# State-space stage and recurrent output path: the order of a feature tile's, a scan step's and an output's parts dealt anew

## The chip, the cores and the metric

The kernel runs on one core of a Trainium2 chip. It has TensorE (PE) for matrix products, VectorE (DVE), ScalarE (ACT) and GpSimd (POOL) for the rest, and SyncE (SP), which here only issues transfers. The metric is the device time of one execution in microseconds, the median of several.

## What is computed

Three blocks over a sequence of 1024 positions and 1024 features, in float32: a gated linear attention block with an MLP, a hybrid block (state-space and differential attention), and a block with a convolution and a gated recurrence. The change touches the state-space half of the second block and the recurrence of the third. Of the reference, cut:

```python
# second block, state-space half
z, xbc, dt_f, dt_b, q, k, v, g = jnp.split(h @ w_in, offs, axis=-1)
xbc = silu(centred_dwconv(xbc, conv_w, conv_b))            # 5 taps, 1536 features
xs, Bm, Cm = split(xbc)                                    # 1024, 2 x 128, 2 x 128
# ssd_chunked, both directions; chunks of 128, 16 heads of 64 in 2 groups
a_cs = cumsum(dt * A)
decay = exp(where(lower, a_cs[l] - a_cs[s], -inf))
y_diag = einsum(cb[..., None] * decay, x * dt)             # cb = C B^T
chunk_states = einsum(Bm, x * dt * decay_to_end)
prev = scan(dec * h + st)                                  # over 8 chunks
y_off = einsum(Cm, prev) * exp(a_cs)
y = y_fwd + y_bwd + D * xs
y_ssm = rms_norm(y * silu(z))                              # per group
# third block, recurrence: 8 heads of 128, y_hgrn = rms_norm(o) * silu(zg)
S_new = exp(b_last)[..., None] * S + einsum(k_dec, v); o = o_inter + o_intra
```

## The kernel before, in words

Every stage of the kernel is written as one generator per engine, with names like `pe_ssm_scan`, `act_ssm_scan`, `dve_ssm_scan`. A generator issues some instructions and yields; a yield is a slot. `weave` merges generators of one engine by weight: the one with the smallest (slots taken + 0.5) / weight goes next. So the order of each engine's queue is fixed when the program is built, by where the yields stand. Each engine works its queue strictly in order and waits on semaphores by events (`at["silu", m]`). Rings of buffers (`e.take`) make the taker wait until the last holder's readers are done; `hold` keeps a buffer out of the ring until `drop`. `PB` and `PD` are rings of 4 PSUM banks each; `Acc` has 2 buffers of 128x1024, `Xw` and `Wr` one, `Er` 6, `Dr_` and `Zr` 3. Between stages all engines meet at a fence. Products with weights (`fm`, `tm`) use three passes with high and low parts; `act_unit` and `dve_unit` (L312, L321) split the next weight tile, one unit ahead.

The state-space stage (`ssm_stage`) runs:

1. `steps_` (dt, cumulative sums, decays: `dA`, `acs`, `wd`, `ea`) woven with `dense(0)`: feature tiles m = 8 (B), 10 (C), 0, 1. For a tile: two products on TensorE (`fm`, one for each half of the sequence), pad copies on ScalarE (L1544), tap 0 there (L1549), four taps on VectorE (L1594), SiLU (L1557), then for m < 10 eight transposes on TensorE and two copies out (L1563), for m = 10, 11 the products C B^T and their copies (L1570).
2. For i = 0 to 3 (four heads each): the scan of 8 steps, woven with a side part: the dense part of i + 1 and the gate of i (`tm` products L211 into "z2", SiLU L1837). A step n has four slots. TensorE: "st" (states), "off", "seg" of n + 1, "Y". ScalarE: exponential (L1695) and the scaled triangles for n + 2 (L1691). VectorE: `values` (adds Y, L1765), new state (L1786, L1790), L times W (L1798) and times C B^T (L1801) which is G, "yo" (L1808) and two y1 adds (L1814). GpSimd: xw (L1721, L1723), W (L1729, L1732), skip products (L1739). GpSimd's part is woven with nothing.
3. After i = 1 and 3 the output of the group: squares (L1870), mean (L1882), root (L1891), scale (L1884), transposes, gain (L1876) into `Acc`, stores to `ym_scratch` by SP. The output of group 0 is woven with the first 8 slots of the dense part of i = 3 (tile 6).

In the scans there are in this order the tiles 2, 3; then 9, 11, 4, 5; then 6 (mostly in the output part) and 7; scan 3 has only its gate.

The recurrent stage (`rec_stage`) weaves for each head h the recurrence of h (weight 42), the output path of h - 1 (`*_rec_out`, 18) and the dense part of h + 1 (10). In `rec`, seven levels l: differences on VectorE (L2832, L2834), exponential (L2754), z on GpSimd (L2794, L2796), products on TensorE (`lv`), a predicated copy (L2846). The output path: square (L554), mean (L558, L560), root (L564), scale (L568, "hn"), transposes ("hoT"), gate product (L2910), store.

Of the kernel before, what the change touches and what calls it, by code (L numbers as in the profile page):

```python
# [17 lines left out]
NT = 8  # L18
# [209 lines left out]
def program(nc, A, out, ctx):  # L228
# [1178 lines left out]
    def pe_ssm_steps(e):  # L1407
# [9 lines left out]
        pe_done(u)  # L1417
        b = e.take(PB, "dt", hold=True)
# [76 lines left out]

    def pe_ssm_dense(e, i):
        for cols, ms in dense_ms(i):
            u = pe_unit(e, W2in, cols)
            for mi, m in enumerate(ms):
                for th in range(2):  # L1500
                    fm(e, u, mi * 128, th, 2, "xbc", m, th)
                    yield
                for j in range(1, 5):
                    yield
                if m < 10:
                    dst = Acc.of("xbc", m)
                    for th in range(2):
                        b = e.take(PB, "xbcT", m, th)
                        e.wait_ge(*at["silu", m])
                        ins = transposed(e, b, [dst[:, tile(th * 4 + j)] for j in range(4)])  # L1510
                        ins.then_inc(*at.inc("pe", "xbcT", m, th))
                        yield
                    if m < 8:
                        at.also("pe", ("xbc", m))
                else:
                    BT, CT = Acc.of("xbc", m - 2), BC[m - 10][0]
                    e.wait_ge(*at["silu", m - 2])
                    e.wait_ge(*at["silu", m])
                    for th in range(2):
                        b = e.take(PB, "cb", m - 10, th)  # L1520
                        for j in range(4):
                            sl = tile(th * 4 + j)
                            ins = mms(e, b[:, j * 128:(j + 1) * 128], [(BT[:, sl], CT[:, sl])])
                        ins.then_inc(*at.inc("pe", "cb", m - 10, th))
                    at.also("pe", ("xbc", m - 2))
                    yield
            pe_done(u)
# [4 lines left out]

    def act_ssm_dense(e, i):
        g = i // 2
        CT, CB, Bt = BC[g]
        for _, ms in dense_ms(i):
            act_unit(e)
            for m in ms:
# [3 lines left out]
                for th in range(2):  # L1542
# [3 lines left out]
                    yield  # L1546
# [4 lines left out]
                for j in range(1, 5):  # L1551
                    yield
# [5 lines left out]
                if m < 10:  # L1558
                    for th in range(2):
                        o = XS[i % 2][:, th * 4:th * 4 + 4, (m % 2) * 128:(m % 2) * 128 + 128] if m < 8 else \  # L1560
                            Bt[:, th * 4:th * 4 + 4, :]
                        e.wait_ge(*at["xbcT", m, th])
                        e.copy(o, four(PB.of("xbcT", m, th))).then_inc(  # L1563
                            *at.inc("act", "xs", m, th, free=("xbcT", m, th)))
                        yield
                else:
                    at.also("act", ("xbc", m))
                    for th in range(2):
                        e.wait_ge(*at["cb", g, th])
                        e.copy(CB[:, th * 4:th * 4 + 4, :], four(PB.of("cb", g, th))).then_inc(  # L1570
                            *at.inc("act", "CB", g, th, free=("cb", g, th)))
                    Acc.drop("xbc", m - 2)
                    yield
                if m // 2 != 4:
                    Acc.drop("xbc", m)

# [5 lines left out]

    def dve_ssm_dense(e, i):
        for _, ms in dense_ms(i):
            dve_unit(e)
            for m in ms:
                for th in range(2):
                    yield
                a = Acc.of("xbc", m)
                for j in range(1, 5):  # L1590
# [5 lines left out]
                    yield  # L1596
                if m < 10:
                    for th in range(2):
                        yield
                else:  # L1600
                    g = m - 10
                    for th in range(2):
                        e.wait_ge(*at["CB", g, th])
                    e.wait_ge(*at["dtsp"])
                    for tt in range(NT):
                        e.wait_ge(*at.last("dve"))
                        e.tensor_tensor_reduce(out=dCB[:, :], in0=BC[g][1][:, tt, :], in1=ident[:, :], scale=1.0,
                                               scalar=0.0, op0=MUL, op1=ADD, accum_out=cbd[:, tt:tt + 1]).then_inc(
                            *at.inc("dve", "cbd", g, tt))
                    hs = slice(8 * g, 8 * g + 8)  # L1610
                    e.wait_ge(*at["D"])
                    e.wait_ge(*at["cbd", g, 7])
                    e.tensor_tensor(esk[:, :, hs], dt_[:, :, hs], bc(cbd[:, :].unsqueeze(2), [128, 8, 8]),
                                    MUL).then_inc(*at.inc("dve", "esk0", g))
                    e.wait_ge(*at["esk0", g])
                    e.tensor_tensor(esk[:, :, hs], esk[:, :, hs], bc(Dr[:, hs].unsqueeze(1), [128, 8, 8]),
                                    ADD).then_inc(*at.inc("dve", "esk", g))
                    yield
# [1752 lines left out]
```

## Time and profile before

| | |
|---|---|
| runs | 4748.28, 4752.44, 4752.59 us, median 4752.44 |
| profiled execution | 4753.36 us, span 4751.6 |
| busy, share of the span | PE 82%, DVE 46%, ACT 36%, POOL 11% |
| state-space stage | 1433.3 to 2045.5 us |
| recurrent stage | 3596.6 to 4263 us |

Times in the rows are microseconds from the start of the span; "L211" is a line of the kernel, and many products have that line because one helper issues them. "Idle before" with an arrow names the instruction that ended a wait. PEclk, the granted clock, is a share of 2.4 GHz; its two levels are 1.0 and 0.5.

### The profile page before, as it was taken

How to read it: one execution, taken by the hardware profiler on the slowest of the kernel's cores; microseconds unless marked ns; L12 is line 12 of the kernel's file. 1: busy time of each engine (PE TensorE's matmuls, PEld its weight loads, DVE VectorE, ACT ScalarE, POOL GpSimd, SP SyncE). 2: the span in 40 equal slices, each digit the busy share in tenths (PEclk: the TensorE clock that was granted, in tenths of full speed). 3: DMA queues.
4: the chain of work that ended last, by engine and by line, in shares of the span. 5: the costliest groups of instructions: out<-in, count | busy, mean ns of one | idle time of the engine just before them, and what ended most of it. 6: DMA issues, size and time to landing. Idle time of an engine off the chain costs nothing.

```text
span 4751.6 us, 49011 instructions
## 1 busy us (share of the span) xinstructions
PE 3899.8 (82%) x20470; PEld 3212.4 (68%) x20470; DVE 2203.3 (46%) x2728; ACT 1702.4 (36%) x2231; POOL 516.9 (11%) x450
## 2 busy tenths in 40 slices
PE   6977699999956876878888876957877989869988
PEld 5865677878744655666666655945655777757988
DVE  3333333443463454434544553259993555553222
ACT  3322132112113443445655652123444454521122
POOL 0000001001020333300000000020002232320001
PEclk8977899999978888989999997978998999978999
DMA  2221211111111000010101003111111101014111
GB/s 79 72 80 58 106 49 54 45 45 45 53 41 33 26 18 27 18 45 25 31 23 33 23 14 141 42 54 49 58 54 36 40 28 38 29 50 155 36 43 61
DMA packets 196850, 232.32 MB, mean 49 GB/s; under 512 B 8391, under 2 KB 168084, under 8 KB 196628
## 3 DMA queue, kind: packets, MB, share of 16 engines
q1 hardware_dynamic: 190868, 208.20, 13.3%
q10 hardware_dynamic: 5760, 20.97, 1.1%
q8 instruction: 162, 2.65, 0.2%
q14 instruction: 60, 0.49, 0.0%
HBM read 185.10 MB, written 44.04 MB: 48 GB/s over the span
## 4 chain that ended last, share of the span: by engine, by line
PE 57%; DVE 20%; ACT 10%; issue 8%; POOL 2%; DMA 2%; SPq 0%; ACTq 0%; DVEq 0%; POOLq 0%
PE pd L211 48%; PE pq L211 6%; DVE t L2410 5%; DVE t L2188 2%; ACT t L2136 2%; DVE t L321 2%; PE pd L355 2%; ACT t L312 1%; DVE t L1327 1%; PE pq L355 1%; DVE t L1594 1%; DVE t L511 1%; POOL t L564 1%; DMA t<-ym_scratch 0%; DVE t L540 0%
## 5 line engine op out<-in xcount | busy, mean ns | idle before, releaser
L211 PE MATMUL pd<-t 128*128 128x512 f32 (+2 forms) x15920 | 3137.2, 358 | 147.4 <-DVE t L582 55.1
L211 PEld LDWEIGHTS pd<-t 128*128 128x128 f32 x15920 | 2590.8, 194 | 647.7 <-issue 190.9
L211 PE MATMUL pq<-t 128*128 128x128 f32 (+5 forms) x3222 | 636.7, 370 | 284.3 <-ACT t L2440 50.2
L211 PEld LDWEIGHTS pq<-t 128*128 128x128 f32 (+2 forms) x3222 | 435.5, 205 | 431.5 <-issue 91.8
L312 ACT ACTIVATE t<-t 128x2048 fp32r<-128x2048 f32 (+2 forms) x130 | 240.4, 1849 | 725.4 <-PE pd L211 695.3
L321 DVE TENSOR_TENSOR t<-t 128x2048 fp32r<-128x2048 f32 (+2 forms) x130 | 304.9, 2346 | 348.5 <-ACT t L312 348.4
L355 PE MATMUL pd<-t 128*128 128x128 f32 x960 | 161.5, 324 | 205.6 <-DVE t L485 59.8
L2410 DVE SCALAR_TENSOR_TENSOR t<-t 128x1024 f32<-128x1024 f32 x240 | 307.7, 1283 | 11.9 <-ACT t L2400 5.4
L355 PEld LDWEIGHTS pd<-t 128*128 128x128 f32 x960 | 138.8, 170 | 233.6 <-issue 66.4
L1278 DVE TENSOR_TENSOR t<-pd,t 128x512 f32<-128x512 f32 x256 | 172.2, 690 | 127.9 <-PE pd L211 127.9
L355 PE MATMUL pq<-t 128*128 128x128 f32 x356 | 67.3, 345 | 186.5 <-DVE t L568 77.9
L355 PEld LDWEIGHTS pq<-t 128*128 128x128 f32 x356 | 55.3, 182 | 197.1 <-DVE t L568 80.0
L2136 ACT ACTIVATE t<-t 128x1024 f32<-128x1024 f32 x128 | 146.2, 1144 | 94.2 <-DVE t L2193 94.1
L1267 DVE TENSOR_TENSOR t<-t 128x512 fp32r<-128x512 f32 x64 | 44.4, 693 | 276.4 <-POOL t L1250 276.4
L611 DVE TENSOR_TENSOR t<-pd,t 128x512 f32<-128x512 f32 x64 | 44.3, 692 | 271.2 <-PE pd L211 271.2
L2188 DVE CUSTOM_DVE_ANT_0 t<-pq,t 128x1024 f32<-128x1024 f32 x128 | 151.3, 1220 | 28.7 <-PE pq L211 21.7
L1250 POOL TENSOR_TENSOR t<-t 128x512 f32<-128x512 f32 x64 | 66.5, 1040 | 628.4 <-ACT t L1229 628.4
L1229 ACT ACTIVATE t<-pd 128x512 f32<-128x512 f32 x64 | 38.4, 599 | 258.1 <-PE pd L211 258.1
L2794 POOL TENSOR_TENSOR t<-t 128x512 f32<-128x512 f32 x56 | 80.7, 1441 | 453.1 <-ACT t L2754 425.4
L2846 DVE COPY_PREDICATED t<-t,pq 128x512 f32<-128x512 int32 x128 | 90.5, 735 | 80.5 <-PE pq L211 79.4
L2328 POOL TENSOR_TENSOR t<-t 128x4 f32<-128x4 f32 x2 | 2.5, 1254 | 1081.0 <-DVE t L1319 1081.0
L1594 DVE SCALAR_TENSOR_TENSOR t<-t 128x1024 f32<-128x1024 f32 x48 | 68.1, 1420 | 95.2 <-ACT t L1549 93.9
(268 smaller groups left out, 2799.5 us busy)
## 6 DMA issues: line engine op xcount, KB each, us to landing
t<-in_w_in_dram SPq DMA_DIRECT2D x89, 512.0 KB, 5.0
t<-in_w_mlp_dram SPq DMA_DIRECT2D x32, 1024.0 KB, 5.3
t<-in_w_in_dram SPq DMA_DIRECT2D x20, 1024.0 KB, 5.4
t<-in_w_out_dram SPq DMA_DIRECT2D x20, 1024.0 KB, 5.2
t<-ym_scratch ACTq DMA_DIRECT2D x24, 512.0 KB, 8.7
ym_scratch<-t SPq DMA_DIRECT2D x20, 512.0 KB, 2.6
t<-in_x_dram SPq DMA_DIRECT2D x16, 512.0 KB, 4.7
gs_scratch<-t SPq DMA_DIRECT2D x16, 512.0 KB, 2.7
```

The costliest lines, as they stand in the source:

```text
L211: ins = e.matmul(out, l, r, start=(first and j == 0), stop=(last and j == n - 1), skip_group_check=True)
L312: e.activation(WH[i % 2][:, 0:z], WR[i % 3][:, 0:z], ACT.Copy).then_inc(*at.inc("wh", "wh", i))
L321: e.tensor_tensor(WL[i % 3][:, 0:z], WR[i % 3][:, 0:z], WH[i % 2][:, 0:z].bitcast(F32), SUB).then_inc(*at.inc("wl", "wl", i))
L355: ins = e.transpose(b[:, j * 128:(j + 1) * 128], s, ident[:, :])
L1250: e.tensor_tensor(q[:, :], r[:, :], r[:, :], MUL).then_inc(*at.inc("pool", "q", j, m, th, free=("r", j, m, th)))
L1278: e.tensor_tensor(X1[:, tt, half(nh)], PD.of("down", j, tt, nh)[:, :], X1[:, tt, half(nh)], ADD).then_inc(*at.inc("dve", "xadd", j, tt, nh ...
L1594: e.scalar_tensor_tensor(a[:, :], pad2[:, j:j + S], pc("cw2", 12 * j + m), a[:, :], MUL, ADD).then_inc(*at.inc("dve", "conv", m))
L2136: e.activation(s[:, r, :], s[:, r, :], ACT.Exp, bias=x[:, 2 + r:3 + r], accum_out=x[:, 4 + r:5 + r]).then_inc(*at.inc("act", "sexp", h, tt))
L2188: e.tensor_tensor_reduce(out=s[:, r, :], in0=PQt[r][:, :], in1=bias[:, 896 - 128 * tt:896 - 128 * tt + 1024], scale=0.125, scalar=-3.0e38, ...
L2410: e.scalar_tensor_tensor(a[:, :], p[:, k:k + S], taps(k, g), a[:, :], MUL, ADD).then_inc(*at.inc("dve", "ctaps", g))
L2794: e.tensor_tensor(v4(z[:, :], w_)[:, :, 0, :], v4(k[:, :], w_)[:, :, 0, :], v4(dd[:, :], w_)[:, :, 0, :], MUL).then_inc(*at.inc("pool", "h ...
L2846: e.copy_predicated(At[:, th * 4:th * 4 + 4, :], bc(Mi[:, l:l + 1, :], [128, 4, 128]), four(PB.of("lv", h, l, th))).then_inc(*at.inc("dve" ...
```

## The change

In the dense part, `pe_ssm_late` and `act_ssm_late` do the transposes (or C B^T) and copies of the tile before, after the products and tap 0 of the tile at hand; the last tile of a dense part gets them in `*_dense_end`, which in a scan comes after the first two of the gate's four slots. C B^T is in two slots. VectorE's diagonal (`dve_ssm_diag`) comes after the next tile's taps. Per tile there are 8 slots throughout. In a scan step the quarters are dealt anew: TensorE does "Y" of n - 1 first, VectorE does `values(n - 1)` after G, GpSimd runs straight through with xw two steps ahead of W's predecessor, skips one step earlier. The output's ScalarE squares come before the side part, its transposes three slots later. The recurrent output path is spread over more slots, with mean and scale apart and its `Dr_` buffer held from its first slot until the mean. SP's generators follow the slots; GpSimd issues no transfers.

```diff
@@ pe_ssm_steps
         pe_done(u)
+        yield
         b = e.take(PB, "dt", hold=True)
@@
+    def pe_ssm_late(e, m):
+        for th in range(2):
+            if m is None:
+                pass
+            elif m < 10:
+                b = e.take(PB, "xbcT", m, th)
+                e.wait_ge(*at["silu", m])
+                transposed(e, b, [Acc.of("xbc", m)[:, tile(th * 4 + j)] for j in range(4)]).then_inc(
+                    *at.inc("pe", "xbcT", m, th))
...
+            yield
@@ pe_ssm_dense
                 for th in range(2):
                     fm(e, u, mi * 128, th, 2, "xbc", m, th)
                     yield
-                for j in range(1, 5):
-                    yield
-                if m < 10:
-                    dst = Acc.of("xbc", m)
...
-            pe_done(u)
+                if mi == 1:
+                    pe_done(u)
+                yield from pe_ssm_late(e, before_m(i, m))
+                yield from idle(4)
+
+    def pe_ssm_dense_end(e, i):
+        yield from pe_ssm_late(e, last_m(i))
@@ act_ssm_dense
                     e.copy(pad2[:, 2 + th * 512:2 + th * 512 + 512], PD.of("xbc", m, th)[:, :]).then_inc(
                         *at.inc("act", "xpad", m, th, free=("xbc", m, th)))
-                    yield
+                    if th == 0:
+                        yield
...
-                for j in range(1, 5):
-                    yield
+                yield
+                yield from act_ssm_late(e, i, before_m(i, m))
+                yield from idle(3)
                 dst = a if m < 10 else CT
@@ dve_ssm_dense
-                for th in range(2):
-                    yield
+                yield from idle(4)
                 a = Acc.of("xbc", m)
...
+                if (before_m(i, m) or 0) >= 10:
+                    dve_ssm_diag(e, i // 2)
+                yield
@@ pe_ssm_scan
         for n in range(8):
-            if n < 6:
-                states(n + 1)
+            if n:
+                values(n - 1)
+            yield
+            if n < 6:
+                states(n + 1)
             yield
@@ act_ssm_scan
             yield
             yield
+            yield
             Er.drop("Rf", i, n)
-            yield
@@ pool_ssm_scan
         moved(0)
-        yield
-        for n in range(8):
-            if n < 7:
-                moved(n + 1)
-            yield
-            yield
-            if n < 4:
-                skip(n)
-                skip(7 - n)
-            yield
-            yield
+        weights(0)
+        moved(1)
+        skip(0)
+        skip(7)
+        for n in range(7):
+            if n < 5:
+                moved(n + 2)
+            weights(n + 1)
+            if n < 3:
+                skip(n + 1)
+                skip(6 - n)
@@ dve_ssm_scan
         for n in range(8):
-            if n:
-                values(n - 1)
             if n < 7:
@@
             yield
+            if n:
+                values(n - 1)
+            yield
             if n:
                 e.wait_ge(*at["ea"])
@@ act_ssm_out
+        yield from idle(4)
         for m in range(4):
             a = e.take(Acc, "yT", g, m)
@@ pe_ssm_out
+        yield from idle(3)
         e.wait_ge(*at["yn", g])
@@
-    def ssm_side(e, i, gate, dense):
+    def ssm_side(e, i, gate, dense, end):
+        gated = gate(e, i)
         if i < 3:
             yield from dense(e, i + 1)
-        yield from gate(e, i)
+            yield from islice(gated, 2)
+            yield from end(e, i + 1)
+        yield from gated
@@ ssm_stage
-        weave((steps_(e), 31), (dense(e, 0), 31))
+        weave((steps_(e), 32), (dense(e, 0), 32))
+        steps(end(e, 0))
@@
-            weave((scan(e, i, ytok), 33), (side, [20, 35, 12, 4][i]))
+            weave((scan(e, i, ytok), 33), (side, [22, 38, 14, 4][i]))
@@
-                weave((out_(e, i // 2), 5), (islice(side, 8), 9))
+                weave((out_(e, i // 2), 10), (islice(side, 8), 8))
@@ act_rec_out
+        s = Dr_.of("hsq", h)
         e.wait_ge(*at["hO", h, 1])
-        yield
-        s = Dr_.of("hsq", h)
         e.vacant(Dr_, "hsq", h)
         act_heads(e, 8, four8(s), O3[:, :, :], "rec", h)
-        yield from idle(4)
+        yield from idle(7)
@@ dve_rec_out
-        yield
-        s = Dr_.take(("hsq", h))
+        s = Dr_.take(("hsq", h), hold=True)
+        yield
         dve_heads_mean(e, 8, 128, four8(s), 1e-6, "rec", h)
+        at.also("dve", ("hsq", h))
+        Dr_.drop("hsq", h)
+        yield
+        yield
         dve_heads_scale(e, O3[:, :, :], 8, 128, "rec", h)
-        at.also("dve", ("hsq", h))
@@ pool_rec_out
         yield
+        yield
         pool_heads(e, 8, "rec", h)
-        yield from idle(4)
+        yield from idle(5)
@@ pe_rec_out
-        yield
-        yield
-        yield
+        yield from idle(4)
         for th in range(2):
@@ rec_stage
-                parts.append((out_(e, h - 1), 18))
+                parts.append((out_(e, h - 1), 16))
```

## Rows read from the trace of the kernel before

**Rows 1.** The page, part 1: busy time, share of the span and instructions of TensorE.

```profile
PE 3899.8 (82%) x20470; PEld 3212.4 (68%) x20470; DVE 2203.3 (46%) x2728; ACT 1702.4 (36%) x2231; POOL 516.9 (11%) x450
```

**Rows 2.** Windows: us, busy (count) by engine, granted clock, DMA share, GB/s.

```profile
1433.30:1545.40 112.10, 72.09 (x294) 53.77 (x294) 33.35 (x46) 35.17 (x51) 2.87 (x8) 0.79 0.11 33
1545.40:1649.80 104.40, 87.74 (x457) 70.95 (x458) 52.96 (x68) 46.13 (x90) 41.01 (x39) 0.90 0.05 16
1649.80:1802.60 152.80, 117.85 (x577) 95.52 (x577) 73.00 (x99) 61.51 (x112) 38.50 (x34) 0.87 0.06 21
1802.60:1847.40 44.80, 19.12 (x89) 15.43 (x88) 13.65 (x8) 20.21 (x41) 9.02 (x5) 0.72 0.19 71
1847.40:1937.90 90.50, 75.88 (x400) 61.04 (x400) 46.17 (x65) 42.42 (x92) 36.42 (x38) 0.91 0.06 15
1937.90:2020.10 82.20, 66.86 (x344) 51.20 (x344) 39.89 (x59) 36.43 (x78) 33.71 (x34) 0.88 0.04 11
2020.10:2045.50 25.40, 5.32 (x34) 5.08 (x33) 7.61 (x7) 11.06 (x24) 1.65 (x1) 0.65 0.20 83
...
3901.60:3981.80 80.20, 69.82 (x395) 60.80 (x396) 44.49 (x54) 39.42 (x42) 21.49 (x15) 0.95 0.12 34
```

**Rows 3.** Waits of TensorE, first part: total, times, longest, in us.

```profile
PE pq L355 <- ACT t L1557: 23.8, 3, 8.3
PE pq L211 <- ACT t L1557: 8.3, 1, 8.3
PE pq L211 <- DVE t L1482: 4.5, 1, 4.5
```

**Rows 4.** Timeline, one feature tile: start, us, engine, line, idle before.

```profile
1498.54 11.16 PE L211 MATMUL pd<-t 128*128 128x512 f32 x48
...
1511.62 5.25 DVE L1594 SCALAR_TENSOR_TENSOR t<-t 128x1024 f32<-128x1024 f32 x4 [6.65 <-ACT t L1549]
...
1518.01 1.97 PE L355 MATMUL pq<-t 128*128 128x128 f32 x8 [8.32 <-ACT t L1557]
```

**Rows 5.** Waits of TensorE, scans 0 to 3 and the output between.

```profile
PE pq L211 <- POOL t L1723: 37.3, 10, 6.6
PE pd L211 <- DVE t L1801: 19.2, 8, 3.8
PE pq L355 <- ACT t L1557: 15.0, 2, 8.2
...
PE pq L211 <- DVE t L1790: 11.4, 4, 5.4
```

**Rows 6.** Timeline, one step of scan 3.

```profile
1961.91 1.18 POOL L1739 TENSOR_TENSOR t<-t 128x256 f32<-128x256 f32 x2
...
1962.62 1.50 DVE L1814 TENSOR_TENSOR t<-t 128x256 f32<-128x256 f32 x2 [1.89 <-POOL t L1739]
...
1964.65 2.07 PE L211 MATMUL pq<-t 128*128 128x256 f32 x4 [3.55 <-POOL t L1723]
```

**Rows 7.** Instructions of L1729, state-space stage: duration ns min/median/max, first and last start.

```profile
L1729 POOL TENSOR_TENSOR t<-t x32: 1032/1545/1548, 1544.2 to 2007.3; 128x512 f32<-128x512 f32 x32
```

**Rows 8.** Timeline, output of group 0.

```profile
1808.20 0.59 ACT L1544 COPY t<-pd 128x512 f32<-128x512 f32 x1 [3.06 <-PE pd L211]
...
1821.78 1.97 PE L355 MATMUL pq<-t 128*128 128x128 f32 x8 [13.62 <-DVE t L1884]
...
1836.14 1.26 ACT L1876 ACTIVATE t<-pq,t 128x512 f32<-128x512 f32 x2 [2.68 <-DMA ym_scratch<-t]
```

**Rows 9.** Waits of TensorE, recurrent stage with heads 1 to 7.

```profile
PE pq L355 <- DVE t L568: 50.6, 7, 8.1
```

**Rows 10.** Timeline, start of a recurrent head.

```profile
3970.57 2.05 PE L211 MATMUL pq<-t 128*128 128x128 f32 x16 [1.71 <-POOL t L2796]
...
3976.33 1.25 POOL L2796 TENSOR_TENSOR t<-t 128x512 f32<-128x512 f32 x1
...
3980.72 1.09 PE L355 MATMUL pq<-t 128*128 128x128 f32 x4 [8.11 <-DVE t L568]
```

More of the change, by code:

```diff
@@ L1492, in dve_ssm_steps, with before_m, last_m @@
         e.tensor_tensor(flat(wd), flat(wd), flat(dt_), MUL).then_inc(*at.inc("dve", "wd"))
+    def before_m(i, m):
+        ms = [m_ for _, part in dense_ms(i) for m_ in part]
+        n = ms.index(m)
+        return ms[n - 1] if n else None
+    def last_m(i):
+        return 2 * i + 1
+    def pe_ssm_late(e, m):
[7 more added lines that the diff above has]
+                    *at.inc("pe", "xbcT", m, th))
+                if m < 8 and th == 1:
+                    at.also("pe", ("xbc", m))
+            else:
+                BT, CT = Acc.of("xbc", m - 2), BC[m - 10][0]
+                e.wait_ge(*at["silu", m - 2])
+                e.wait_ge(*at["silu", m])
+                b = e.take(PB, "cb", m - 10, th)
+                for j in range(4):
+                    sl = tile(th * 4 + j)
+                    ins = mms(e, b[:, j * 128:(j + 1) * 128], [(BT[:, sl], CT[:, sl])])
+                ins.then_inc(*at.inc("pe", "cb", m - 10, th))
+                if th == 1:
+                    at.also("pe", ("xbc", m - 2))
+            yield
     def pe_ssm_dense(e, i):
@@ L1623, in sp_ssm_dense @@
             for m in ms:
-                for _ in range(8 if m < 10 else 7):
-                    yield
+                yield from idle(8)
     def x_ready(i):
@@ L1656, in states, with values @@
                 *at.inc("pe", "st", i, n, free=("xw", i, n)))
+        def values(n):
+            for ev in x_ready(i):
+                e.wait_ge(*at[ev])
+            b = e.take(PD, "Y", i, n)
+            e.wait_ge(*at["G", i, n])
+            for j in range(4):
+                ins = mms(e, b[:, j * 64:j * 64 + 64], [(Er.of("Rf", i, n)[:, j, :], XS[i % 2][:, n, j * 64:j * 64 + 64])])
+            ins.then_inc(*at.inc("pe", "Y", i, n, free=("Rf", i, n)))
         front(0)
@@ L1885, in dve_ssm_out @@
             *at.inc("dve", "yn", g))
-        for m in range(4):
-            yield
+        yield from idle(8)
     def pool_ssm_out(e, g):
@@ L1918, in ssm_stage @@
             if i != 2:
-                side = ssm_side(e, i, gate, dense)
-            weave((scan(e, i, ytok), 33), (side, [20, 35, 12, 4][i]))
+                side = ssm_side(e, i, gate, dense, end)
+            weave((scan(e, i, ytok), 33), (side, [22, 38, 14, 4][i]))
             if mul:
@@ L2927, in pe_rec_out @@
             yield
+        yield
     def sp_rec_out(e, h):
-        yield from idle(5)
+        yield from idle(7)
         r = (8 + h) * 128
```

148 lines of the change are left out of this document (61 added, 87 removed).

## The prediction

> **What bounds the kernel now.** The page's first part comes first: TensorE is busy 82% of the span [rows 1]. A share that high still hides 18% idle, so I went to the two stages that the diff touches and cut them where TensorE passes from one part to the next [rows 2]. The state-space stage is the first seven lines, 612.2 us: the steps with the first dense part (112.1), scans 0 and 1 (104.4, 152.8), the output of group 0 (44.8), scans 2 and 3 (90.5, 82.2), the output of group 1 (25.4). TensorE is busy 444.9 of these 612.2 us, the other engines at most 51% of a scan. So no engine is the bound there; TensorE stands at the head of a chain in a fixed order, and what matters is which wait ends last. The last line is one head of the recurrent stage: 80.2 us, TensorE busy 69.8.
>
> In the first part TensorE waits for the SiLU of a feature tile (L1557), 23.8 + 8.3 us in four waits, and 4.5 us for dA (L1482) [rows 3]. One cycle shows why: two products (11.2 us from 1498.54), then TensorE stands 8.32 us while the tile goes through the pad copies, the first tap, four taps on VectorE (5.25 us) and SiLU, then the transposes, and only then the next products [rows 4]. The granted clock is 0.79 of 2.4 GHz over this part, so a good part of it ran at 1.2 GHz, after such waits; scan 2, with few waits, has 0.91 [rows 2].
>
> In the scans and the output between them the waits are: for the second half of GpSimd's xw (L1723) 37.3 us in 10, for G (L1801) 19.2 in 8, for the SiLU 15.0 + 1.4 (8.2 of it in the output), for the new state (L1790) 11.4 in 4 [rows 5]. Without the 8.2 that is 76.1 us. One step of scan 3 shows their cause: GpSimd writes W, then two skip products (end 1963.1), and then xw; VectorE's y1 stands 1.89 us for the skip product, TensorE's state product starts at 1964.65 after 3.55 us for xw [rows 6]. It is a ring: GpSimd's last quarter is wanted first in the next step. The gate's products lie inside this ring and cover nothing of it.
>
> **The change, part by part.**
>
> *First part.* The transposes of tile m now come after the products of tile m+1. The old trace prices the chain from the end of a product to the SiLU's end at 8.3 us, and the new cover is the next tile's 11.2 us. So three of the four waits go (7.1 + 8.3 + 8.3 = 23.8; the last three are 8.3 each and the first is what remains of 32.1). The last tile has no product behind it, so its 8.3 stays. The work after a wait ran at half clock: the products took 13.1 and 12.4 instead of 11.2 us, and three groups of transposes or CB products lose half of theirs: 3.2 + 1.5 back. The acs products stand earlier in the order than dA is ready: FM of tile 8 ends at about 1458.2, dA at 1463.8, so 5.6 instead of 4.5: -1.1. Sum **27.4 us**. Both ends: 22 if the clock gives nothing back; 32 if the last wait went too, which nothing in the order permits.
>
> *The scan step.* No product is added, and TensorE's cyclic order (Y, states, off, seg) is the same; what moves is when the others reach their quarters. GpSimd does xw of step n+2 before W of step n+1, and its skips one step ahead. VectorE adds the values of step n-1 after LWG(n), not before the state. With that each operand is made one step before it is read. A step without gate shows it: after seg(n+1) TensorE has Y(n), the states, off and the next seg, 4.9 us, before it asks for G(n+1), and the exponential (0.6) and both products for G (1.4) take 2.0; after a gate product ScalarE first does the gate's SiLU with two table loads, 5.3 us to G against 6.8 us of products. GpSimd's W (2.6), skips (1.2) and xw (1.5) make 5.3. I went through the new order of all four scans, product by product, with durations of the old trace, and found these waits left: 2.1 us for G in step 0 of scan 1 (its exponential stands behind a pad copy that waits for the second product of tile 9); 3.3 us for G in the last step of scan 3, as before; 1.7 us for xw after the first states of scan 3, because only one Xw buffer exists. The transposes of tile 6 come into scan 2 (1.0), and the start of scan 3 moves 1.0 later, behind the last gate SiLU. So 76.1 - 2.1 - 3.3 - 1.7 - 1.0 - 1.0 = 67.0. VectorE has 73.0 us of work in the longest scan against 117.9 of TensorE, GpSimd 38.5 [rows 2]: they fit in sum, but in stretches with conv taps two steps of VectorE take about 15 us where TensorE has 10 and a product. I take 60 and not 67, a tenth for such stretches. Ends: 33, half of the waits come back under another name; 74, all but the 2.0 of moved work.
>
> That the cover must be enough also holds for rings. A tile of Acc is held until its copy out, and two exist: gate 0 and 1 take one before the last tile's copy, gate 2 the other after it. Weight tiles: the order asks for each at least a product after its split. SP's queue holds its weight loads and the stores of ym in the same relative order; a store stands behind no load that waits for later work. No term.
>
> *Output of group 0* (44.8 us). ScalarE's squares now come before the weight split and the pad copy; these stood ahead of them, and the pad copy alone waited 3.06 us [rows 8]. The squares started 4.2 us after the last multiply, and now directly: 4.2 less. Y of step 7 now ends after the last gate product: +1.0, and the first multiply comes after it, +0.4. After the first transposes (1821.78) the four output tiles go through one Acc buffer, since the conv tile holds the other: each waits 2.68 us for the store before it and takes 1.26 [rows 8]. The first ends 2.9 us after its transposes, the others every 3.9 us: 14.7, against 19.5 before, when a 7.0 us product stood between the first and second. Then SiLU and the scan's first ScalarE work, 3.5 us, without the 2.6 us of transposes and copies. So 18.2 for 25.6. Sum 4.2 - 1.4 + 7.4 = 10.2, plus 2.0 since the product at half clock moves under the wait of 13.6: **12.2 us**; 12 is taken. Ends 8 and 14. The output of group 1 has no side work: 25.4 stays.
>
> *Recurrent output path.* In seven heads TensorE waits for the scaled head output (L568), 50.6 us in 7 [rows 9], 8.1 in a typical one, from 3972.6 to 3980.7, after 1.71 for the first level [rows 10]. VectorE did mean and scale in one slot with GpSimd's root between, after the exponential of level 1 on ScalarE. Now the square comes before level 0's, the mean before copy 7.1, the scale after level 3's differences, and TensorE has level 1 and a product of 5.7 us before the transposes. What is late next: level 1's z on GpSimd, which ends at 3977.6 [rows 10]; TensorE stands there 5.1-5.3 us instead of 8.1. The transposes then come after Fhq0 at about 3986, the scale ends about 3984.6 behind the root, which stands behind level 2's z in GpSimd's queue. VectorE itself waits some 2.6 us for that root, with cp1, d4 and cp2 behind it; their readers come a product later. Net: 2.9 from the wait, about 1.8 from products at full clock and from overlap, 4.7 per head over six heads, and about 5 in the last head, which has no dense part and in which the wait for mean and root delayed every level. Sum **33 us**. The hold on a Dr_ buffer costs nothing: the mean frees it before level 2's differences ask. Ends: 10 and 50 (all waits).
>
> Sum: 27.4 + 60 + 12 + 33 = 132.4. The profiled execution took 4753.4 (span 4751.6), 0.9 above the median 4752.44; so **4621 us**.
>
> **A rule against it.** In the old trace GpSimd's first W product takes between 1032 and 1548 ns, median 1545 [rows 7], so beside VectorE's products it is half a microsecond longer. The Trainium skill (SBUF — State Buffer, "Who interferes with whom") says that the pair of ports is a lock: a VectorE operation with two SBUF inputs and a GpSimd operation block each other fully. By that rule work moved forward on GpSimd buys nothing where both are dense: the scans' term would be 60 - 28 = 32, the first rival below; by the rows' durations as they stand, stretched ones included, it is the 60 above.
>
> **Rivals.**
> *GpSimd and VectorE take turns.* A step alone is then their sum, some 4.5 + 2.8 = 7.3 us by the shortest durations, about what a step without gate took. About 12 steps have neither products nor gate; each would stay 2.3 above TensorE's 5.0: 28 us less, 4649. For it: W's 1545 median. Against: VectorE's operations on PSUM, half of its step, are not stretched, and its wait for a skip is a matter of order. The rule above gives this time.
> *The recurrent wait changes its name.* VectorE stands for the root, and all of the 33 comes back at levels 1 to 3: 4654. For: the root moves behind a longer queue. Against: the product Fhq0 now lies between.
> *The scans keep half,* with exponentials, copies of late tiles and table loads in ScalarE's one queue: 4648.
> *Slower: late tiles block TensorE.* A late transpose has the whole order of products behind it. In scans the taps are dealt over two steps, so a tile may need 17 us and more. If it is late behind its successor's product, all engines stall. For a loss the eight late tiles in scans must each cost 132/8 = 17 us more than the order found above, that is come some 17 us after TensorE asks. Nothing in the rows gives this: a tile's chain is 8.3 alone.
>
> **Chances.** Forecast 0.60 (its own range 4603-4640), turns 0.15, recurrent 0.08, half 0.08, larger than forecast 0.05 (all waits gone: 32 + 74 + 14 + 50 = 170, 4583), slower 0.03, about same 0.01. The range 4590 to 4672 takes the rivals and the low ends of two parts together (22 + 33 + 8 + 20 = 83, 4670). Faster by over 0.2% (9.5 us, about what a measurement of this kernel can tell): 0.96; within 0.01; slower 0.03.
>
> **What the new profile would show.** The first part some 85 us, with one wait of 8 for L1557. In scans TensorE's wait for L1723 from 37 to under 8, for L1801 under 8. Scan 0 and 1 near 89 and 123 us, the output of group 0 near 33. In a head, no wait for L568, and one of 5 for L2796. I am wrong if the waits for L1801 or L1695 grow as those for L1723 fall, or if the granted clock in the scans stays at 0.87-0.91.

## The result and the profile after

After the change the kernel takes 4600.85 us (median of 4, 4599.04 to 4603.68) against 4751.84 for the kernel before in the same rounds: ratio 0.9684, 95% interval 0.9667 to 0.9701. That is 151.0 us less; the forecast was 132 less (4621), in its range of 4590 to 4672.

The kernel's lines have moved: the SiLU of a tile is L1594 (was L1557), xw L1751 (L1723), G L1829 (L1801), the new state L1818 (L1790), the triangles L1720 (L1691), dA L1483 (L1482), the values of a step L1795 (L1765), the scale of the group's output L1915 (L1884), z of a level L2833 (L2796), the differences of a level L2869 and L2871 (L2832, L2834).

The windows of the same eight stretches as in [rows 2], with the same columns:

```profile
1429.30:1511.40 82.10, 65.85 (x294) 49.46 (x294) 33.53 (x46) 34.32 (x51) 2.83 (x8) 0.88 0.17 52
1511.40:1595.90 84.50, 82.05 (x457) 67.48 (x458) 53.81 (x67) 46.07 (x90) 42.95 (x39) 0.98 0.04 13
1595.90:1717.00 121.10, 112.69 (x580) 92.21 (x580) 72.75 (x99) 61.35 (x113) 40.62 (x34) 0.93 0.08 27
1717.00:1749.30 32.30, 17.18 (x79) 14.24 (x77) 16.46 (x10) 18.41 (x38) 11.93 (x5) 0.75 0.26 98
1749.30:1829.90 80.60, 73.73 (x408) 60.04 (x408) 48.48 (x65) 43.50 (x94) 38.05 (x38) 0.93 0.06 16
1829.90:1892.50 62.60, 57.69 (x344) 47.41 (x344) 43.83 (x59) 36.88 (x78) 34.04 (x34) 0.98 0.05 14
1892.50:1917.80 25.30, 5.72 (x33) 5.43 (x33) 7.29 (x5) 11.05 (x24) 1.65 (x1) 0.63 0.20 83
...
3893.40:3968.90 75.50, 69.54 (x391) 59.94 (x390) 44.36 (x51) 39.22 (x43) 22.45 (x15) 0.95 0.12 35
```

Line by line against [rows 2]: the first part 112.1 to 82.1, scans 0 and 1 104.4 and 152.8 to 84.5 and 121.1, the output of group 0 44.8 to 32.3, scans 2 and 3 90.5 and 82.2 to 80.6 and 62.6, the last output unchanged. The state-space stage went from 612.2 to 488.5. TensorE's busy time fell too, 444.9 to 414.9, with the same products: more of it ran at the upper clock (0.98 in scans 0 and 3). Each execution also scatters by a few us in code that the change does not touch: the state-space stage began at 1433.3 and now begins at 1429.3.

A head of the recurrent stage takes 75.5. The line of before with 80.2 in [rows 2] is not one head: it runs from the start of one head's transposes (3901.62) to the end of the next head's first ones (start 3980.72 [rows 10], 1.09 long), so one head was 79.1. From the transposes of k in head 0 to those in head 6, six heads took 476.4 us before (3704.6 to 4181.0) and take 453.3 now (3577.3 to 4030.6), 3.9 less each.

TensorE's waits in the first part:

```profile
PE pq L355 <- ACT t L1594: 7.5, 1, 7.5
PE pq L211 <- DVE t L1483: 5.8, 1, 5.8
```

In scans and output (1511.4 to 1892.5), where [rows 5] had 37.3 for xw and 19.2 for G:

```profile
PE pq L211 <- ACT t L1720: 19.0, 4, 10.6
PE pd L211 <- DVE t L1829: 10.9, 4, 4.6
PE pq L355 <- DVE t L1915: 3.9, 1, 3.9
PE pq L211 <- DVE t L1818: 3.3, 2, 2.5
PE pq L211 <- POOL t L1751: 2.1, 2, 1.3
PE pd L211 <- DVE t L1795: 0.8, 1, 0.8
```

No wait for a SiLU is left in a scan. The first line is the wait for the triangles at the start of a scan; it was 11.6 in 4 before (L1691) and has grown, 10.6 of it at scan 2, behind the output of group 0. And in one recurrent head, where [rows 9] had some 8 for the scale:

```profile
PE pq L211 <- POOL t L2833: 5.1, 1, 5.1
...
PE pq L355 <- DVE t L568: 0.2, 1, 0.2
```

### The profile page after: what moved, and what is told of

It is laid out like the page before. It is cut to its first block, busy times and chain, and to the rows that moved or that the text cites. A ratio compares the mean times of both kernels' runs of the same rounds, so it can differ in the third digit from the quotient of the medians.

```text
span 4597.1 us, 48973 instructions
## 1 busy us (share of the span) xinstructions
PE 3863.9 (84%) x20470; PEld 3187.3 (69%) x20470; DVE 2217.1 (48%) x2728; ACT 1700.9 (37%) x2231; POOL 532.2 (12%) x450
## 4 chain that ended last, share of the span: by engine, by line
PE 57%; DVE 20%; ACT 10%; issue 8%; DMA 2%; POOL 2%; SPq 0%; ACTq 0%; DVEq 0%; POOLq 0%
PE pd L211 49%; PE pq L211 6%; DVE t L2447 6%; ACT t L2173 2%; DVE t L2225 2%; DVE t L321 2%; PE pd L355 2%; ACT t L312 1%; DVE t L1327 1%; PE pq L355 1%; DVE t L511 1%; DMA t<-ym_scratch 0%; DVE t L1637 0%; DVE t L540 0%; DVE t L2243 0%
## 5 line engine op out<-in xcount | busy, mean ns | idle before, releaser
L211 PE MATMUL pq<-t 128*128 128x128 f32 (+5 forms) x3222 | 619.4, 365 | 257.5 <-ACT t L2477 49.5
L211 PEld LDWEIGHTS pq<-t 128*128 128x128 f32 (+2 forms) x3222 | 424.4, 202 | 398.3 <-issue 79.5
L2447 DVE SCALAR_TENSOR_TENSOR t<-t 128x1024 f32<-128x1024 f32 x240 | 307.7, 1284 | 11.9 <-ACT t L2437 5.4
L2173 ACT ACTIVATE t<-t 128x1024 f32<-128x1024 f32 x128 | 146.2, 1144 | 94.2 <-DVE t L2230 94.1
L2225 DVE CUSTOM_DVE_ANT_0 t<-pq,t 128x1024 f32<-128x1024 f32 x128 | 151.3, 1220 | 30.3 <-PE pq L211 23.3
L2791 ACT ACTIVATE t<-t 128x1024 f32<-128x1024 f32 x56 | 59.3, 1059 | 100.8 <-DVE t L2871 100.5
```

The lines of the kernel that those rows point to most:

```text
L211: ins = e.matmul(out, l, r, start=(first and j == 0), stop=(last and j == n - 1), skip_group_check=True)
L2173: e.activation(s[:, r, :], s[:, r, :], ACT.Exp, bias=x[:, 2 + r:3 + r], accum_out=x[:, 4 + r:5 + r]).then_inc(*at.inc("act", "sexp", h, tt))
L2225: e.tensor_tensor_reduce(out=s[:, r, :], in0=PQt[r][:, :], in1=bias[:, 896 - 128 * tt:896 - 128 * tt + 1024], scale=0.125, scalar=-3.0e38, ...
L2447: e.scalar_tensor_tensor(a[:, :], p[:, k:k + S], taps(k, g), a[:, :], MUL, ADD).then_inc(*at.inc("dve", "ctaps", g))
L2791: e.activation(Dr_.of("d", h, l)[:, :], Dr_.of("d", h, l)[:, :], ACT.Exp).then_inc(*at.inc("act", "hde", h, l))
```

## The experiments

Differences are between medians. The kernel before stood at 4748.8 to 4751.8 in the groups of runs, and each ratio has an interval of about 0.0013 to either side, some 6 us; a smaller difference of times decides nothing by itself, and the trace is asked. In stretches that an edit leaves alone the traces agree more closely (from scan 0's first state copy to the first square of group 1 it is 376.4, 376.4, 376.5 and 376.7 us after and in runs 1, 7 and 8), so the length of such a stretch decides more than the whole time. "Slower" without more is against 4600.85.

**1. Recurrent output path undone.** The five `*_rec_out` and the weight of `rec_stage` as before.

```diff
-                parts.append((out_(e, h - 1), 16))
+                parts.append((out_(e, h - 1), 18))
```

> The kernel after, with the recurrent output path in its old slots; the state-space stage stays new. Theory (the traces' shares): the recurrent stage gives back 4.5 us in each of six heads and 0.8 in the last, 27.8, so about 4628 us. Rival (the two stages are not independent, or part of the 27.8 was scatter between executions): 4605 to 4620. If the term of the forecast, 33, had been right, 4634.

4624.81 us (0.9742, 0.9729 to 0.9755): 24.0 slower. Its trace has the 50.6 us in 7 for L568 of [rows 9] again. The traces agree with the times: from the transposes of k in head 0 to those in head 6 it takes 476.6 us (before 476.4, after 453.3), 23.3 more, and the last head 0.8 more. So the recurrent part is worth 24, neither the 27.8 of my theory (its 4.5 a head is about what the 80.2 gives when it is read as one head) nor the 33 of the sum. The rest, 124 by the trace and 127 by the times, is the state-space stage.

**2. Only the scan steps new, on the kernel before.** The four scan generators of the kernel after, and

```diff
-            steps(pool_ssm_scan(e, i))
+            pool_ssm_scan(e, i)
```

> The kernel before, with only the four engines' new scan steps; feature tiles, outputs and the recurrent stage stay old. Theory (the ring of xw, state and G made most of the scans' waits): TensorE's waits for xw (37.3 us) and the new state (11.4) go and those for G (19.2) halve, with some 5 to 10 us of clock, 55 to 68 less: 4684 to 4697. The SiLU waits stay. Rival (the steps gain only together with the tiles pipelined, since a tile that is waited for stops the ring anyway): 30 or less, 4720 or more. Rival (GpSimd and VectorE take turns): about 35 less, 4717.

4724.86 us (0.9948, 0.9936 to 0.9961): only 24.0 faster than before, and my theory fell; the time is that of the first rival (30 or less). From the first copy of the new state in a scan to that in the next (or to the first square) the four scans took 111.1, 146.0, 89.6 and 79.5 us in the kernel before, and 110.0, 148.7, 83.1 and 63.4 here. Scan 3, which has no feature tile, gained 16.1, scan 2 with one tile 6.5; scans 0 and 1, full of tiles, gained nothing (1.1 less and 2.7 more). TensorE's waits there (1548.3 to 1807), against 17.8 for xw, 12.5 for G, 10.0 for the state and 8.2 for SiLU before:

```profile
PE pq L355 <- ACT t L1557: 32.6, 5, 8.9
PE pd L211 <- DVE t L1805: 9.6, 4, 3.8
PE pq L211 <- ACT t L1557: 6.9, 1, 6.9
```

The waits for xw and state are gone, and 39.5 us for a tile's SiLU stand in their place. In scan 0 of the kernel before, TensorE stands for xw and finds the tile's transposes ready behind it:

```profile
1577.49 2.08 PE L211 MATMUL pq<-t 128*128 128x256 f32 x4 [4.42 <-POOL t L1723]
...
1580.72 0.60 PE L355 MATMUL pq<-t 128*128 128x128 f32 x4
```

Here xw is ready, so TensorE comes to the same transposes earlier, and stands there:

```profile
1575.37 1.09 PE L355 MATMUL pq<-t 128*128 128x128 f32 x4 [5.19 <-ACT t L1557]
```

A tile's chain of 8.3 us [rows 4] was there all the time; TensorE's stand for xw, earlier in its queue, hid it.

**3. Scan steps old, everything else new.** The reverse, on the kernel after.

```diff
-            pool_ssm_scan(e, i)
+            steps(pool_ssm_scan(e, i))
```

> The kernel after, with the four scan generators of before; tiles, outputs and the recurrent path stay new. Theory (the shares add): 55 to 68 us slower than after, 4656 to 4669. Rival (steps and tiles each cover the same waits, so that one alone already has most of the gain): under 40 slower, under 4640. Rival (they need each other): over 80 slower, 4681 or more.

4643.37 us (0.9778, 0.9765 to 0.9791): 42.5 slower, between my theory (55 to 68) and the first rival (under 40). The steps are worth 24 on the old tiles and 42.5 on the new ones. Run 1's 24.0 and run 4's 12.0 taken off the 105.4 that this kernel is faster than before leave some 69 for the tiles alone. By the measure of run 2 the scans take 102.5, 116.7, 87.4 and 77.1 here, 42.5 less than in the kernel before, 29.3 of it in scan 1; the rest is about what the first part gained. But the new tiles alone leave most of the ring: TensorE still waits 28.0 us in 8 for xw (37.3 before), 11.5 for G and 7.1 for the state, and no longer for a SiLU. So each of the two parts shortens the scans, and the rest of the gain needs both: by this measure it is 21.0 us for the steps alone, 42.5 for the tiles alone and 85.9 together.

**4. Output functions and their weave old.** The added idle slots of the `*_ssm_out` functions taken out, and

```diff
-                weave((out_(e, i // 2), 10), (islice(side, 8), 8))
+                weave((out_(e, i // 2), 5), (islice(side, 8), 9))
```

> The kernel after, with the output functions and their weave as before (squares behind the weight split and the first pad copy, first transposes between the products), tiles and steps new. Theory (the squares' place and the output's tail are the 12 us of the forecast): 8 to 13 us slower, 4609 to 4614. Rival (the late transposes of the tiles alone, which moved two groups of them and a wait out of the output, made the gain): 0 to 4 slower.

4612.89 us (0.9711, 0.9698 to 0.9724): 12.0 slower. TensorE stands 13.6 us for the scale of the output again, as in [rows 8]. In the trace 9.8 of the 12.0 stand at this place: 4.6 until the first square and 5.2 from there to scan 2's first state copy; the other 2 are within the scatter of the times. Term and mechanism hold.

**5. Which engine's step matters.** Three kernels. First, only GpSimd's order old:

```diff
         moved(0)
-        weights(0)
-        moved(1)
-        skip(0)
-        skip(7)
-        for n in range(7):
-            if n < 5:
-                moved(n + 2)
-            weights(n + 1)
-            if n < 3:
-                skip(n + 1)
-                skip(6 - n)
+        yield
+        for n in range(8):
+            if n < 7:
+                moved(n + 1)
...
+            if n < 4:
+                skip(n)
+                skip(7 - n)
```

(The old `moved` makes xw and then W.)

> The kernel after, with only GpSimd's order of a scan step as before (xw of the next step, then W, then skips, and xw of the one after only behind them); TensorE and VectorE keep the new quarters. Theory (xw as GpSimd's last quarter closes the ring): TensorE waits for xw again in the steps without a gate, 25 to 37 us and some clock, 4628 to 4645. Rival (VectorE's values behind G are what opened the ring): 8 us slower or less, under 4609. By take-turns no difference, 4601, since GpSimd's work is the same.

4632.19 us (0.9755, 0.9741 to 0.9768): 31.3 slower; TensorE waits 27.8 us in 9 for xw. Second, only VectorE's values in their old place:

```diff
         for n in range(8):
+            if n:
+                values(n - 1)
             if n < 7:
                 s_new, s_old = St[(n + 1) % 2], St[n % 2]
...
             yield
-            if n:
-                values(n - 1)
             yield
```

> The kernel after, but VectorE adds the values of step n-1 before the new state, as before, and not behind G; TensorE and GpSimd stay new. Theory (every operand must be made a step early): VectorE then stands for Y, which TensorE has only just started, and G comes 3.3 us after Y's end where TensorE has 3.1 us of states, off and seg: 0.2 to 0.7 per step, 5 to 20 us in all, 4606 to 4621. Rival (GpSimd's place is all of the ring): no difference, 4601.

4602.13 us (0.9692, 0.9679 to 0.9705): 1.3 slower, no difference, against my theory; the four scans take 340.6 us together, 340.3 after. Third, GpSimd new, the others old (`pe_ssm_scan`, `act_ssm_scan` and `dve_ssm_scan` of before):

```diff
         for n in range(8):
-            if n:
-                values(n - 1)
-            yield
             if n < 6:
                 states(n + 1)
...
```

(This is TensorE's part; Y of step n comes at the end of the step again.)

> The kernel after, with the scan steps of TensorE, ScalarE and VectorE as before and only GpSimd's order new. It splits the 42.5 us that all four old cost: GpSimd's old order alone had cost 31, VectorE's values in their old place nothing. Theory A (the new quarters of TensorE and VectorE matter only together, each operand a step early): 8 to 14 us slower than after, 4609 to 4615. Theory B (GpSimd's order is the whole of the ring; the 11 us are what old GpSimd and old VectorE cost together): 0 to 3 slower, 4601 to 4604.

4629.00 us (0.9744, 0.9731 to 0.9757): 28.2 slower, and both theories missed. What had moved on TensorE was not only a name. Its cycle (Y, states, off, seg) is the same, but all of it now stands one slot later against the side's products. TensorE's timeline of that kernel at step 2 of scan 0 (merged rows name the shape that came first: x32 are Y's 8 of 128x64, then 24 of tile 3's first product):

```profile
1539.93 1.88 PE L211 MATMUL pq<-t 128*128 128x512 f32 x4
1547.13 9.00 PE L211 MATMUL pd<-t 128*128 128x64 f32 x32 [5.33 <-DVE t L1826]
```

and of the kernel after, at the same place (x32 are the product's 24 of 128x512, then Y's 8):

```profile
1537.23 1.88 PE L211 MATMUL pq<-t 128*128 128x512 f32 x4
1538.54 6.90 PE L211 MATMUL pd<-t 128*128 128x512 f32 x32
```

In both the first row is seg. In the kernel after, the product comes between seg and Y and covers G; with the old slot Y comes first and TensorE stands 5.33 us. Over scans and output it waits 21.0 us in 10 for G there, against 10.9 in 4, and 6.8 for the state against 3.3. By the measure of run 2 scan 0 takes 106.1 against 92.3, scan 3 69.8 against 61.4, and scans 1 and 2 2.7 more together. Old GpSimd costs 31, old slots of the others 28, both 42.5: not 59, since again each hides part of the other. VectorE's values belong to neither by themselves. Run 5's third kernel put back the slots of TensorE, ScalarE and VectorE together: the timeline shows TensorE's phase at work in one place, and how the 28 are shared among the three engines is open.

**6. GpSimd's first W product written twice.** 32 more of them.

```diff
+            e.tensor_tensor(w[:, :, :], bc(Ust[:, :].unsqueeze(1), q4), bc(ddt[:, n, hs].unsqueeze(2), q4),
+                            MUL).then_inc(*at.inc("pool", "W0b", i, n))
```

> The kernel after, with the first W product of GpSimd written twice: 32 more products of 1.0 to 1.5 us, 32 to 48 us more on GpSimd in the scans, nothing else. Theory (GpSimd has slack, and VectorE is not on the path while it is stretched): 0 to 8 us slower, under 4609. Rival (GpSimd and VectorE take turns, and a step is their sum): most of the 32 to 48 us shows where no product and no gate lie, at least 15 us, 4616 or more.

4606.70 us (0.9702, 0.9689 to 0.9715): 5.9 slower for 32 to 48 us of added work. Scan 3, the kernel after and then this one:

```profile
1832.80:1894.20 61.40, 54.93 (x336) 45.97 (x336) 44.91 (x61) 34.01 (x71) 34.04 (x34) 0.97 0.00 1
```

```profile
1841.50:1902.90 61.40, 54.94 (x336) 45.97 (x336) 49.05 (x61) 34.01 (x71) 43.06 (x41) 0.96 0.00 1
```

GpSimd has 9.0 us more, VectorE 4.1 us more for the same 61 instructions, and the scan takes 61.4 us in both. So the engines do stretch each other, and it costs nothing here. The rival, which asked for 15 us or more, is out. What shows is 7.2 us by the traces, 4.9 of it in scan 0 and 0.9 each in scans 1 and 2.

**7. Root before z of level 2.**

```diff
         yield
-        yield
         pool_heads(e, 8, "rec", h)
-        yield from idle(5)
+        yield from idle(6)
```

> The kernel after, with GpSimd's root of the recurrent output path before the z of level 2, not behind it. Theory (in the last head, without a dense part, the scale stands for the root that stands for z of level 2, and TensorE waits 6.4 us for it): 5 to 7 us less, 4594 to 4596; the six heads before stay at 75.6, since there the product covers it. Rival (the wait is made by the scale itself, stretched beside z): 0 to 2 less. Rival (the root before z delays level 2 in every head): 0.3 to 1.7 us per head more, 4603 to 4613.

4598.64 us (0.9684, 0.9671 to 0.9697): 2.2 less, undecided by the times (the ratio is that of the kernel after). The last head, in the kernel after:

```profile
4065.24 1.63 POOL L564 TENSOR_TENSOR t<-t 128x8 f32<-128x8 f32 x1
4066.84 1.24 POOL L2831 TENSOR_TENSOR t<-t 128x512 f32<-128x512 f32 x1
4066.91 2.27 DVE L568 TENSOR_TENSOR t<-t 128x1024 f32<-128x1024 f32 x1 [2.76 <-POOL t L564]
...
4069.32 1.09 PE L355 MATMUL pq<-t 128*128 128x128 f32 x4 [6.40 <-DVE t L568]
```

and here:

```profile
4060.09 2.08 POOL L564 TENSOR_TENSOR t<-t 128x8 f32<-128x8 f32 x1
...
4064.13 2.29 DVE L568 TENSOR_TENSOR t<-t 128x1024 f32<-128x1024 f32 x1
...
4066.57 1.08 PE L355 MATMUL pq<-t 128*128 128x128 f32 x4 [3.20 <-DVE t L568]
```

The wait for the root (2.76) is gone, half of TensorE's stays: it is the scale's own place, behind level 3's differences, and its own 2.29 us. From the first level's products (4046.83, here 4046.90) to the transposes of k (4092.41, here 4090.65) the head is 1.8 shorter, and the six heads before it are 1.1 shorter together. That is the first rival's size (0 to 2), not the theory's 5 to 7: half of the wait was the root's, the other half the scale's.

**8. Cumulative sums five slots later.** In `pe_ssm_steps`, `act_ssm_steps`, `dve_ssm_steps`:

```diff
-        yield
+        yield from idle(6)
         b = e.take(PB, "acs", hold=True)
```

> The kernel after, with the products of the cumulative sums and what reads them five slots later on TensorE, ScalarE and VectorE, behind the first product of tile 10. Theory: the wait of 5.8 us for dA is covered, and the product behind it runs at full clock, 1.3 more: 7 less, 4594. Rival (the first part is bound by the chain of a tile, and the wait comes back at the transposes or at the start of scan 0): 0 to 3 less.

4595.48 us (0.9676, 0.9663 to 0.9690): 5.4 less. The wait for dA is 0.3 us instead of 5.8. From the first pad copy of the stage (1450.78; after 1447.62) to scan 0's first state copy (1513.6; 1517.8) it is 62.8 us instead of 70.2, 7.4 less; the stage itself began 3.2 later in this execution, in code that is the same. The theory holds, and so does its 7.

**9. A version beyond both.** Runs 7 and 8 together, and the output tiles of group 0 written where their transposes have left y (SP's stores read them there):

```diff
-            a = e.take(Acc, "yT", g, m)
+            a = y[:, :, tile(m)] if g == 0 else four8(e.take(Acc, "yT", g, m))
...
-                e.wait_ge(*at["yT", 0, 3, 1])
+                for m in range(4):
+                    e.wait_ge(*at["ym2", m])
```

> The kernel after with three edits: products of the cumulative sums five slots later (measured alone: 5.4 less), root of the recurrent path before z of level 2 (alone: about 2 less), and the output tiles of group 0 written into the place of y that their transposes have just left, not into the one free Acc buffer; GpSimd's skips of scan 2 wait for the four stores. Theory (the stores through one Acc buffer hold ScalarE three times 2.7 us, and the SiLU and the triangles of scan 2 stand behind them; VectorE's taps end at 1740.6 and bound what can be had): 5 us from the third, 4588 in all. Rival (the stores in pieces of 512 bytes land so late that skips and y stand for them): the third costs 0 to 10, 4593 to 4603.

4583.52 us (0.9650, 0.9637 to 0.9663): 17.3 less than after, the fastest of all measured. The wait for the triangles at scan 2 is 6.4 instead of 10.6:

```profile
1733.48 1.06 ACT L1594 ACTIVATE t<-t 128x1024 f32<-128x1024 f32 x1 [1.94 <-DVE t L1637]
1734.44 4.77 ACT L1720 ACTIVATE t<-t 128x128 f32<-128x128 f32 x16
1737.02 4.30 PE L211 MATMUL pq<-t 128*128 128x512 f32 x8 [6.36 <-ACT t L1720]
```

The SiLU now waits for VectorE's taps, not for stores. From the first square to scan 2's first state copy it is 30.1 us, was 36.2: 6.1 from this edit. With the 7.4 and 2.9 that the traces show for the two others that makes 16.4; the other 0.9 is no more than medians of different runs scatter.

**10. A product before level 1.** On top of run 9, in `pe_rec`'s levels (and two slots given back behind levels 2 and 3; the output's transposes, gate product and store one slot later):

```diff
         def back(l):
+            if l == 1:
+                yield
+                yield
             for th in range(2):
```

> The kernel of the run before this one, and in the recurrent stage TensorE does the first product of the second weight pair before level 1 and not behind it; the transposes of the head output, the gate product and its store one slot later. Theory (the wait of 5.1 us for z of level 1 is covered by a product of 5.7, and the levels after it come at the pace of their chain, some 2 us of it back): 3 us in each of six heads, 18 less, 4570. Rival (the levels form one chain of difference, exponential, z and copy, so that the wait only moves to level 2): 0 to 5 less, 4583 to 4588.

4582.67 us (0.9647, 0.9634 to 0.9660): 0.9 less than run 9, nothing. The rival has the time right, but not quite the place: TensorE's waits in the stage for z went from 41.7 to 33.2 us, and the 9.4 for L568 went; 12.5 + 3.4 us in 13 for the gate product of the head before (`hy`, L2962 there; 1.8 in run 9) came in. The covered wait came back mostly as another.

## Why the prediction was right, and where its sizes were off

*What bounds it.* Right: a chain in fixed order, not an engine. GpSimd took 9 us more in a scan without a change of its length (run 6).

*The sum.* Forecast 132.4, measured 151.0. The terms missed in both directions: the scans brought 21 us more than forecast, the recurrent path 9 less. So the time came nearer than the terms, and that part is luck.

*First part.* Forecast 27.4, measured 30.0. TensorE's waits fell from 36.6 [rows 3] to 13.3, 23.3 less, and its busy time from 72.1 to 65.9, 6.2 less. The last SiLU wait (7.5 for 8.3) and dA's 5.6 (5.8) came as said; the clock gave 1.5 more than counted.

*Scans.* Forecast 60, measured 81.1 (429.9 to 348.8). This is the term that was mis-sized. The waits counted as 76.1 are 17.1 now (10.9 + 3.3 + 2.1 + 0.8): 59.0 gone, where the walk through the order had 67 and I took 60. But TensorE's busy time over the four scans fell from 348.3 to 326.2, 22.2 us, and 59.0 + 22.2 = 81.2 (busy time times granted clock, summed over the four scans, is 309 before and 310 after: the same work). The step that failed is the one that turns waits into time: the first part and the output got a clock term, the scans none, though [rows 2] showed 0.87 to 0.91 there. Now it is 0.93 to 0.98, as the prediction's own sign asked; its other sign, under 8 us for G, failed: 10.9.

The attribution was off too, and the sum hid it. "Ring of GpSimd's last quarter" explains 24 us alone; in scans 0 and 1 the tiles' chains stood behind the same waits (run 2), and the new tiles alone shorten the scans by 42.5 (run 3). The sentence that TensorE's cyclic order is the same and only the others' quarters move left out that TensorE's slots moved against the side's products: up to 28 us hang on this (run 5, where ScalarE's and VectorE's old slots came back with TensorE's). A union of waits from one trace priced the whole change well, and would have priced its parts badly: by [rows 5] the steps alone should have brought some 60.

The one G wait named for scan 1 (2.1) is 2.8 us in the trace; that in the last step of scan 3 (3.3) is 2.4; the largest, 4.6 in scan 2, was not foreseen. The one for xw in scan 3 (1.7) is 1.3.

*Output of group 0.* Forecast 12, measured 12.5 and, undone, 12.0 (run 4). TensorE's waits in it fell from 25.7 to 15.3 us: the 13.6 for the scale are 3.9 now and the 8.2 for a SiLU are gone, but 10.6 for scan 2's triangles stand where 3.1 stood. That is the tail through one Acc buffer, and it is there as priced: 17.9 us from the first transposes to scan 2's first product, forecast 18.2. Run 9 writes the tiles elsewhere and gains 6.1.

*Recurrent path.* Forecast 33, measured 24.0 by times (run 1) and 23.9 by the traces. Six heads gained 3.9 each, not 4.7, with a wait of 5.1 for z of level 1 as said. The waits did their part: over the six heads TensorE's fell from 60.9 to 35.9 us, 4.2 a head, more than the 2.9 counted, since the 1.7 for the first level [rows 10] went too. What failed is the 1.8 a head from "products at full clock and from overlap": TensorE's busy time did not fall at all (415.6 to 417.1, granted clock 0.95 and 0.96). The last head gained 0.8, not 5 (46.4 to 45.6): there no product lies between levels, so the scale, now two levels later in its queue and behind a root that stands behind z, is waited for again, 6.4 us. The rival "the wait changes its name" was right for this one head, and right again for the attempt in run 10.

*Take turns.* Against: run 6, and scan 3, where a step without a gate product takes 4.3 us (the first row of such a step starts at 1855.24, that of the next at 1859.58); that rival had 7.3. The durations do show the rule of the Trainium skill (SBUF — State Buffer, "Who interferes with whom") at work: VectorE's scale L568, with two SBUF inputs, took 1225 ns in all eight heads before, and has a median of 2284 now that it runs beside z on GpSimd. GpSimd's turn to stand comes in the output of group 0, where a second half of xw, 0.61 us elsewhere, lasts as long as VectorE's scale beside it:

```profile
1726.57 4.83 DVE L1915 TENSOR_TENSOR t<-t 128x4096 f32<-128x4096 f32 x1 [1.76 <-POOL t L1921]
1727.08 4.79 POOL L1751 TENSOR_TENSOR t<-t 128x256 f32<-128x256 f32 x1
```

The rule agrees on the stretch; it says nothing about whether the stretched engine is waited for.

## What to carry to other kernels

A wait in a trace names one chain, and while an engine stands for it, what comes later in its queue gets ready unseen. Before pricing one part of a change, list the other chains that the engine will ask for next and their lengths: the longest of them is what remains when the named wait goes. And when waits in front of TensorE go in many places, add what its work at half clock gives back, but only where the granted clock of the same stretch leaves room: it was 30.0 of the 123.7 us that the state-space stage gained (0.87 to 0.91 in its scans before), and nothing in the recurrent heads, which stood at 0.95. When generators are woven, moving one by a slot moves all its instructions against the side work, whose products are the cover.

## What the runs showed of the hardware

Two things that I had not expected in this size. The clock: with the same work in the four scans (1778 matmul records before, 1789 after), 59 us fewer waits made TensorE's busy time 22 us shorter, and in six recurrent heads 25 us fewer waits made it no shorter (2341 records both times). And the stretch between VectorE and GpSimd is large but uneven, and either engine can be the one stretched (GpSimd's 4.79 us above): 9.0 us more GpSimd work in scan 3 made VectorE's 61 instructions 4.1 us longer, and the second difference of a level (L2871) took 0.69 us alone and 1.75 us beside z in the same head:

```profile
4053.98 0.69 DVE L2871 TENSOR_TENSOR t<-t 128x512 f32<-128x512 f32 x1
...
4058.36 1.71 POOL L2833 TENSOR_TENSOR t<-t 128x512 f32<-128x512 f32 x1
4058.87 1.75 DVE L2871 TENSOR_TENSOR t<-t 128x512 f32<-128x512 f32 x1
```
